# Differential attention: where the score scale is applied, how the row maxima are written, and in which order the first output chunk's tiles are issued

## The reference

```python
q = rope_partial(dq.reshape(b, l, H_D, 2, HD_D), pos)
k = rope_partial(dk.reshape(b, l, H_D, 2, HD_D), pos)
sc = jnp.einsum('bqhcd,bkhcd->bhcqk', qi, k) * scale      # scale = HD_D ** -0.5 = 0.125
p = jax.nn.softmax(jnp.where(mask, sc, NEG_INF), axis=-1)
a = p[:, :, 0] - lam * p[:, :, 1]
od = rms_norm(einsum('bhqk,bkhv->bqhv', a, v), diff_norm_w) * (1.0 - lambda_init)
yc = rms_norm(og, gla_norm_w) * silu(cg)                  # og: GLA output, cg: gate projection
y = jnp.concatenate([yc, yd], axis=-1) @ w_out
```

## Time and profile before

| | before |
|---|---|
| median of three runs | 1226.8 us |
| profiled execution: span, first to last instruction | 1224.7 us |
| what lies around the span (median minus span) | 2.1 us |
| PE busy | 1209.1 us (99%) |
| DVE busy | 725.1 us (59%) |
| POOL busy | 802.0 us (65%) |
| ACT busy | 301.6 us (25%) |
| attention stage of layer 1 | about 703 to 796 us of the span |
| granted TensorE clock, mean | 0.999 |

### The profile page before, as it was taken

The page is one execution under the profiler, slowest core; times in us unless marked ns, Lnnn a source line. Parts: engine busy times, 40 slices in busy tenths (PEclk is TensorE's granted clock), DMA queues, the critical chain, the costliest instruction groups (busy, mean ns, idle before and its releaser), DMA issues.

```text
span 1224.7 us, 23481 instructions
## 1 busy us (share of the span) xinstructions
PE 1209.1 (99%) x8622; PEld 1143.7 (93%) x8622; DVE 725.1 (59%) x1268; ACT 301.6 (25%) x629; POOL 802.0 (65%) x953
## 2 busy tenths in 40 slices
PE   9999999999999999999999998999999999999997
PEld 8987999999999999999999986899999999999997
DVE  6766677776777622217344579676777777741112
ACT  4035332222222200003111167433222222210001
POOL 7962676767676677777654433477777777667772
PEclk9999999999999999999999999999999999999999
DMA  6221222222222233233231301233222222232321
GB/s 222 95 87 36 74 85 96 87 92 86 86 86 86 89 100 90 99 98 111 88 96 54 106 35 35 71 113 96 87 92 86 86 86 86 87 93 98 103 87 73
DMA packets 35993, 108.99 MB, mean 89 GB/s; under 512 B 6161, under 2 KB 8769, under 8 KB 35937
## 3 DMA queue, kind: packets, MB, share of 16 engines
q1 hardware_dynamic: 29232, 102.14, 25.5%
q10 hardware_dynamic: 6704, 6.04, 1.6%
HBM read 103.04 MB, written 5.13 MB: 88 GB/s over the span
## 4 chain that ended last, share of the span: by engine, by line
PE 94%; DVE 2%; ACT 1%; issue 1%; POOL 1%; DMA 0%; ACTq 0%; SPq 0%; POOLq 0%; DVEq 0%
PE psum L630 18%; PE psum L628 12%; PE psum L629 12%; PE psum L631 12%; PE psum L632 9%; PE psum L600 6%; PE psum L602 6%; PE psum L601 6%; PE psum L1131 1%; PE psum L1133 1%; PE psum L1132 1%; PE psum L927 1%; PE psum L868 1%; PE psum L1100 1%; PE psum L907 1%
## 5 line engine op out<-in xcount | busy, mean ns | idle before, releaser
L500 POOL TENSOR_TENSOR w_lo<-w_raw,w_hi 128x512 fp32r<-128x512 f32 x354 | 487.8, 1398 | 14.8
L630 PE MATMUL psum<-h_both,w_hi 128*128 128x480 f32 x704 | 266.8, 379 | 0.0
L453 POOL TENSOR_TENSOR tick<-tick 1x1 f32<-1x1 f32 x183 | 45.1, 247 | 321.0 <-PE psum L632 204.7
L495 POOL TENSOR_SCALAR w_hi<-w_raw 128x512 fp32r<-128x512 f32 x354 | 219.0, 632 | 0.0
L628 PE MATMUL psum<-h_both,w_hi 128*128 128x304 f32 x704 | 215.8, 307 | 0.0
L629 PE MATMUL psum<-h_both,w_hi 128*128 128x304 f32 x704 | 212.6, 302 | 0.0
L631 PE MATMUL psum<-h_both,w_lo 128*128 128x304 f32 x704 | 210.9, 300 | 0.0
L632 PE MATMUL psum<-h_both,w_lo 128*128 128x240 f32 x704 | 191.5, 272 | 0.0
L632 PEld LDWEIGHTS psum<-h_both,w_lo 128*128 128x128 f32 x704 | 132.0, 188 | 20.5
L600 PE MATMUL psum<-h_both,w_hi 128*128 128x272 f32 x488 | 143.8, 295 | 0.0
L602 PE MATMUL psum<-h_both,w_lo 128*128 128x272 f32 x488 | 141.3, 289 | 0.0
(11 more groups left out here) (312 smaller groups left out, 2455.8 us busy)
## 6 DMA issues: line engine op xcount, KB each, us to landing
w_raw<-in_weights SPq DMA_DIRECT2D x184, 512.0 KB, 3.5
x<-in_x SPq DMA_DIRECT2D x8, 272.0 KB, 6.2
w_raw<-in_weights SPq DMA_DIRECT2D x3, 384.0 KB, 5.9
out_diff_v_new<-odd_dv ACTq DMA_DIRECT2D x1, 1024.0 KB, 5.8
out_diff_k_new<-odd_kT ACTq DMA_DIRECT2D x1, 1024.0 KB, 5.0
out_y<-y_one SPq DMA_DIRECT2D x2, 456.0 KB, 2.5
even_rope<-in_rope ACTq DMA_DIRECT2D x1, 544.0 KB, 4.3
odd_rope<-in_rope ACTq DMA_DIRECT2D x1, 544.0 KB, 3.7
```

The lines of the kernel that those rows point to most:

```text
L453: pool.tensor_tensor(tick[:, :], tick[:, :], tick[:, :], ALU.mult).then_inc(ticks, 1)
L495: ins = pool.tensor_scalar(w_hi[:, k, part], w_raw[:, k % RAW, part], 1.0, 0.0, ALU.mult, ALU.add)
L500: ins = pool.tensor_tensor(w_lo[:, k, part], w_raw[:, k % RAW, part], w_hi[:, k, part].bitcast(F32), ALU.subtract)
L630: pe.matmul(two, wh, both[:, :, ONE:T], start=first, stop=False)
```

## The change

Three edits.

1. `rotate` takes a scale. For the four query chunks of differential attention it is 0.125, and the two products become `scalar_tensor_tensor` (times 0.125, times the rotary table) in place of `tensor_tensor`. The exp loses its `scale=0.125`.
2. `odd_max` is one instruction in place of two: the reduce writes its result negated to where the bias is read, and raises `negm` itself. L2064 goes, 20 times, and with it the wait between the two.
3. The fill list: of out chunk 0, tiles 0 to 2 of both halves come first and then tile 3 of both halves. `ODD_FILL` has 3 tiles more at place 1 of step 9, one fewer at place 1 of step 17, and two fewer in step 18 (one at place 1, one at place 2).

```diff
-                    (0, 7, 2), (0, 2, 4), (0, 0, 0), (2, 0, 1), (0, 0, 4), (0, 1, 4), (3, 1, 1), (3, 3, 3),
-                    (2, 1, 4), (0, 4, 2), (0, 5, 0), (0, 5, 3), (0, 0, 1)]
+                    (0, 7, 2), (0, 2, 4), (0, 3, 0), (2, 0, 1), (0, 0, 4), (0, 1, 4), (3, 1, 1), (3, 3, 3),
+                    (2, 1, 4), (0, 4, 2), (0, 4, 0), (0, 4, 2), (0, 0, 1)]
...
-        HALF_TILES = [(item, k) for item in HALVES for k in range(KC if item[0] == "gate" else 4)]
+        FIRST_OUT = HALVES[8:10]
+        HALF_TILES = [(item, k) for item in HALVES[0:8] for k in range(KC)]
+        HALF_TILES += [(item, k) for item in FIRST_OUT for k in range(3)] + [(item, 3) for item in FIRST_OUT]
+        HALF_TILES += [(item, k) for item in HALVES[10:] for k in range(4)]
...
                     ac.activation(d_probs[u % 2][0:nq, c, 0:nk], psum[0:nq, 2 * (u % 2) + c, 0:nk],
-                                  ACT.Exp, bias=sm[:, 4 + c:5 + c], scale=0.125,
+                                  ACT.Exp, bias=sm[:, 4 + c:5 + c],
...
-            def rotate(acc, z, rope, kT, qT_dst):
-
-                o(ve.tensor_tensor(halves(z), pair(acc), halves(rope[:, 0]), ALU.mult))
+            def rotate(acc, z, rope, kT, qT_dst, scale=None):
+
+                if scale is None:
+                    o(ve.tensor_tensor(halves(z), pair(acc), halves(rope[:, 0]), ALU.mult))
+                else:
+                    o(ve.scalar_tensor_tensor(halves(z), pair(acc), scale, halves(rope[:, 0]), ALU.mult, ALU.mult))
                 o.wait()
                 o(ve.stream_shuffle(pair(acc), pair(acc), PARTNER))
                 o.wait()
-                o(ve.tensor_tensor(pair(acc), pair(acc), halves(rope[:, 1]), ALU.mult))
+                if scale is None:
+                    o(ve.tensor_tensor(pair(acc), pair(acc), halves(rope[:, 1]), ALU.mult))
+                else:
+                    o(ve.scalar_tensor_tensor(pair(acc), pair(acc), scale, halves(rope[:, 1]), ALU.mult, ALU.mult))
...
-                        rotate(acc, oz[:, n % 2], o_rope, None, d_qT[:, n - 17])
+                        rotate(acc, oz[:, n % 2], o_rope, None, d_qT[:, n - 17], 0.125)
...
-                o(ve.tensor_reduce(sm[:, 0:2], psum[0:nq, 2 * (u % 2):2 * (u % 2) + 2, 0:nk], AX.X, ALU.max))
-                o.wait()
-                o(ve.tensor_scalar(sm[:, 4:6], sm[:, 0:2], -0.125, None, ALU.mult), negm)
+                o(ve.tensor_reduce(sm[:, 4:6], psum[0:nq, 2 * (u % 2):2 * (u % 2) + 2, 0:nk], AX.X, ALU.max, negate=True),
+                  negm)
```

## The result

In eight runs beside eight of the kernel before, the changed kernel takes 1230.09 us (1229.43 to 1230.54) against 1226.86: a ratio of 1.0025, interval 1.0016 to 1.0034. So it is slower by 0.25%, about 3.2 us, where the forecast was 0.65 us and the range ended at 1228.8. The profiled execution took 1229.61 us with a span of 1227.4, which is 2.7 us over the span before.

What follows compares the result with a forecast made beforehand. PE bounds the kernel, busy 99% of the span. +1.85 at transposes(12) less 1.20 for three tiles gave +0.65 us: span 1224.7 to 1225.35, plus 2.1 makes 1227.45, say 1227.5; range 1226.1 to 1228.8.

Steps and rivals of the forecast that it cites:

- Rotation and negated reduce: On DVE: scaled products and negating reduce cost nothing extra; removing L2064 moves DVE's next instruction forward about 0.19 us.
- Rival C: At the maxima on DVE: the negating reduce costs its 0.20 us, giving 1228.6 us; chance 0.05.
- Units 0 to 11: PE's waits shrink or fill: unit 0 from 0.62 to 0.42, transposes(9) at 742.98, PE at transposes(11) 0.71 us ahead.
- `gate_low(3)` at 1.79 us: Step 10 on DVE: still behind POOL's L482, it ends at 754.43, and o0a3 still waits 1.1 us.
- Rivals B: Step 10: `gate_low(3)` gets ahead of POOL's L482 and takes 0.72 us, giving 1226.4 us; chance 0.12.
- rival D: DVE and POOL order turns at max(8), max(12), max(13), so DVE instructions stand behind POOL's: +2.75, 1229.5 us; chance 0.07.
- o1a0 waits for the sum of o0a: Step 11 fill: o1a0 needs o0a's bank, released by DVE's L2107 at 758.04; PE idles 2.8 us, to 758.10.
- With two tiles, 0.80, transposes(12) start at 758.90: Behind o1a0's wait: two tiles take 0.80 us, so transposes(12) come at 758.90 against 757.05, +1.85 us that stays.
- I price it at 0 to 0.2 us and take 0: Place 0 of step 13: o2a0 comes about level with L2107 of o1a; cost 0 to 0.2 us, taken as 0.
- new idle time after step 13: Sign that the forecast is wrong: PE shows new idle time after step 13.
- -1.20 for three tiles fewer at steps 17 and 18: Three tiles taken early are missing at steps 17 and 18, saving 1.20 us without PE then waiting.
- The sign that I gave 0.08, slower by over 0.2%: Whole kernel: chance 0.08 of being slower beyond the 0.2% band, above 1229.25 us (D and a little).

Runs made afterwards that it cites:

- fill_undone: Changed kernel with the old fill list and table; the scaled rotation and the negated reduce stay. 1225.85 us, ratio 0.9991 against the kernel before.
- scale_later_three: Changed kernel with old fill, `head_scale` moved behind normalise of step h = 3 for the first three blocks only. 1225.04 us, ratio 0.9985.
- wait_filled: Changed kernel with 22 extra, unread matmuls 128x272 in PE's wait in front of o1a0. 1228.39 us, ratio 1.0012.
- one_tile_ahead: Changed kernel with another fill table: one tile ahead instead of three behind step 12, o1a0 behind scores(14). 1225.76 us, ratio 0.9991.
- wait_third_filled: Changed kernel with 8 extra matmuls, 1.0 us of work, in the wait in front of o1a0. 1228.13 us, ratio 1.001.
- two_tiles_later: Changed kernel with two of step 11's four tiles, o1a0 and o1a1, moved to place 1 of step 12. 1226.97 us, ratio 1.0.
- sums_added_sooner: Changed kernel, DVE adding o0a and o0b sums in step 11 right behind normalise(12), before max(13) and `head_low`. 1226.3 us, ratio 1.0.
- fill_alone: Kernel before with only the new fill list and table. 1231.97 us, ratio 1.004.
- filled_o2b_sooner: wait_filled with DVE's sum of o2b moved ahead of normalise(15) in step 14. 1228.59 us, ratio 1.0014.

## Why the prediction was wrong, point by point

- **Rotation and negated reduce: right.** Into SBUF the scaled product takes 725 ns and the plain one 725; into PSUM, which no row had shown, both take 732. The negating reduce of 1024 columns takes 1221 ns, the plain one 1217. Rival C falls, and fill_undone measures what the reduce and the rotation gain together: about 1 us.
- **Units 0 to 11: right.** Idle 0.43 at unit 0 (forecast 0.42), unit 9 at 742.93 without a wait (742.98), unit 11 at 750.96 (750.98). One small miss: 0.26 us idle is left there, so PE came a quarter of a microsecond sooner than my 751.03; it was already 0.28 us sooner at unit 10 (747.05, forecast 747.33).
- **`gate_low(3)` at 1.79 us: right** (end 754.40, forecast 754.43; wait of o0a3 1.05, forecast 1.1). Rivals B and D needed another order of DVE and POOL, which did not occur. scale_later_three shows that B's 0.71 us can be had, by another edit.
- **o1a0 waits for the sum of o0a: right** in place, cause and length: 2.67 us, forecast 2.8; start at 758.15, forecast 758.10.
- **"With two tiles, 0.80, transposes(12) start at 758.90": the step that failed.** PE's wait was priced as its length alone, and everything behind it at the rates of a busy PE. The two tiles took 1.20 us, not 0.80 (758.15 to 759.35), and units 12 to 13 took 5.50 us instead of 4.29, with the granted clock at 0.50 up to 761.9. wait_filled keeps o1a0's wait for DVE and removes the low clock: 1.60 us less at unit 13, of which 0.15 goes back into the wait of o2a0, so 1.45 in the traces and 1.7 us in the medians. Its 1228.39 lies inside the forecast's range. The Trainium skill, TensorE: Matmul & The Clock Gate, Part 1, says that TensorE runs at 1.2 GHz until it has been kept busy and is gated down again when it is not. The trace agrees, with a stretch at 0.50 behind 2.67 us of idle time. I had put the cost of the clock behind the idle time at nothing, without a reason.
- **"I price it at 0 to 0.2 us and take 0": a small miss.** That step named o2a0. At the full clock it does cost 0.15 us (wait_filled, above), within those bounds, but in the changed kernel the low clock hides it, and it was o3b0 that came late, in step 14. That is new idle time after step 13, one of the signs that I had named. The sum of o2b starts at 774.82 behind a normalise of 1.59 us, and o3b0 starts at 775.39. Units 14 to 15 are 5.31 us apart before and in fill_undone, 5.29 in one_tile_ahead, but 5.62 or 5.63 in all five versions of the changed kernel whose list runs three tiles ahead there (after, wait_filled, wait_third_filled, two_tiles_later, sums_added_sooner). So 0.32 us goes with those three tiles. That it is this very wait is read from the traces (0.29 us in fill_alone; gone in filled_o2b_sooner, whose time it did not help).
- **-1.20 for three tiles fewer at steps 17 and 18: right**, 1.14 measured (3.88 at unit 17 to 2.74 at unit 19).

The sum of the profiled execution, then: +1.85 as forecast, +0.45 for what is over it at unit 12 (0.40 in the two tiles, the rest wait), +1.21 to unit 13 at the low clock, +0.37 behind it, 0.32 of that in step 14, -1.14: +2.74. The sign that I gave 0.08, slower by over 0.2%, came, but by none of the mechanisms that I had listed for it. That rival D's 1229.5 lies near the measured time is chance: `head_scale` was ahead of POOL's product as before, and `head_low` took 0.68 us (at 756.97), as at 758.14 in the earlier trace rows.

Open: why the slow stretch was 3.4 us long in one case and 6.8 in the other; whether 1.05 and 0.93 us of idle time sometimes cause one; and about 0.5 us by which the medians (3.2) differ more than the two profiled spans (2.7), which is within the spread of the runs.

## What to carry to other kernels

Before work is taken earlier on the bounding engine, look at what its last piece frees and who frees it: here a PSUM bank was released by a sum that stood three items down in DVE's list, harmless until a tile of the next chunk was put in front of it. Price an idle time of PE twice, as its length alone and with the work behind it at the lower clock: here 1.66 us cost itself alone, and 2.67 us cost itself and 1.5 to 1.7 us more. Where PE must wait anyway, moving useful work into the wait (two_tiles_later), or moving DVE's item forward (sums_added_sooner), gives back 3.1 and 3.8 of the 4.2 us that the new fill cost; the old fill with the same DVE part, 1225.85, is still the better.

## What the runs showed of the hardware

- The granted clock fell to 0.50 behind a wait of 2.67 us that followed one of 1.05, and stayed down 3.4 us. Behind 1.25 and 2.86 us it had fallen before PE started again, and stayed down 6.8 us although PE was busy from 759.32 on. Behind 1.05 and 1.66 us it did not fall.
- Extra matmuls made a kernel faster: 22 of them, 1.7 us.
- The same DVE product, 128x544, takes 0.71 us when it starts ahead of POOL's and 1.79 when POOL's is ahead. The Trainium skill, SBUF — State Buffer, Who interferes with whom, states an exclusive lock between the two engines that the first to issue holds for its whole instruction; both numbers agree with it.
- A reduce that negates costs no more than one that does not (1221 and 1217 ns), and the small instruction that it replaces, 170 ns, held up the next one on DVE by about 0.2 us.
